# Sample rows packed into one operand, one pass over the attention maps, and values' two parts side by side

## The chip, the cores and the metric

The kernel runs on one core of a Trainium2 chip. The time is that of one execution on the device, in microseconds. TensorE (PE) multiplies matrices out of SBUF into PSUM, VectorE (DVE) and ScalarE (ACT) work element by element, GpSimd (POOL) issues the gathers and scatters of the experts, and SyncE (SP) issues the other DMAs. Each engine runs its own list of instructions in order, and they wait for each other by semaphores.

## What is computed

One layer of a streaming encoder for 512 new prompt tokens (x_prompt) and 32 sample tokens (x_sample) that also see 128 cached keys and values. All is float32. D_MODEL is 1024, with 8 heads of two 64-wide query and key maps and 128-wide values. The part that the change touches:

```python
def diff_attend(q, k, v, mask, lam):
    s = jnp.einsum('bqhmd,bkhmd->bhmqk', q, k).astype(jnp.float32) * ATTN_SCALE
    s = jnp.where(mask, s, -jnp.inf)
    p = jax.nn.softmax(s, axis=-1)
    a = p[:, :, 0] - lam * p[:, :, 1]
    return jnp.einsum('bhqk,bkhv->bqhv', a.astype(v.dtype), v)
...
    h = rms_norm(x, norm_mix_g)
    z = h @ w_in
    u_pool, q, k, v, gate_logits = jnp.split(z, IN_SPLITS, axis=-1)
    q = rope_partial(q.reshape(B, T, N_HEADS, 2, HEAD_DIM), pos)
    k = rope_partial(k.reshape(B, T, N_HEADS, 2, HEAD_DIM), pos)
...
    attn = (rms_norm(attn, subln_g) * (1.0 - lam_init)).reshape(B, T, V_WIDTH)
```

Beside it stand a pooling branch, sigmoid gates for both branches, an output projection, a choice of 2 of 16 experts for each token, and a last norm.

## The kernel before

Every float32 product is made of three matmuls: both operands are split into a high part that TensorE takes exactly (F32R) and the low rest, and `three` adds high x high, high x low and low x high in PSUM. ScalarE copies the high part, VectorE subtracts it from the original to get the low part. Both do this for each chunk of weights that SyncE loads (wh, wl out of rawA), through four slots.

The 544 tokens stand in five tiles of 128. Tiles 0 to 3 are the prompt. Tile 4 holds the last 96 prompt tokens once more and then the 32 sample tokens; only the latter are used of it.

The stages are the norm and its transposes, the pooling branch and its gates, the eight heads, the second gates (gate blocks 0 to 7), the two branches' projections, the output projection, the choice of experts and the experts.

In the stage of the heads, TensorE projects head h (`project(h, j)`, j over 8 rows of weights, in each all five tiles x three matmuls of 384 columns: q, k and v) while the attention of head h-1 runs in between. `turn` transposes q and k of head h-1. `scores(g, t)` makes both maps of query tile t, `turn_probs(g, t)` transposes the combined map, and `values(g, t)` multiplies it with the values, block by block of 128 keys: 1, 2, 3, 4 and 2 blocks for the five tiles, 12 per head. The last two tiles of a head are finished inside the next head's `project(h, 0)` and `project(h, 1)`, ahead of that head's `turn`.

VectorE's `step(g, s)` first combines the maps of tile s-1: reciprocal of both sums, times lambda (L1071), one pass over the first map (L1073), and one that adds the second (L1074). Then it finds the maximum of tile s (nb). Then it makes the low part of the transposed map (atl). Then it clamps the finished tile s-2 and sums its squares (L1090, L1091). ScalarE's `step` squares the finished tile once more at a small scale (bsq), copies it to att, copies the transposed map (ath), and takes the exponentials of tile s with their sums (E, esum). Two sums of squares are kept, for values of ordinary and of huge size.

Around it, for each head: ScalarE copies the five projected tiles to qkv (L737), VectorE applies rotary (L1104 to L1109), ScalarE and VectorE make the high and low parts of v, q and k, and each head's four weight chunks are split at four places (`nxt(3)` to `nxt(6)`). The last head's attention has the gate blocks of TensorE around it in place of a projection. The order is written out by hand; heads 2 to 6 are one loop.

## Time and profile before

| | us |
|---|---|
| median of three runs (943.45 to 947.93) | 946.29 |
| the profiled execution | 945.17 |
| its span | 943.2 |
| TensorE busy | 851.2 |
| VectorE busy | 603.1 |
| ScalarE busy | 505.3 |

The span is the profiled execution from its first to its last instruction; about 2 us of the time lie around it. The granted clock of TensorE is 0.96 of full speed over the whole, and 1.00 in the stage of the heads (132 to 480 us). PE is the list of matmuls, PEld that of their weight loads. A matmul's recorded duration overlaps with its neighbours' because they are pipelined, so the distances between starts tell what one costs. In the timeline a bracket gives the idle time in front of an instruction and who ended it.

### The profile page before, as it was taken

The numbers are of one execution on the slowest core, as the hardware profiler recorded it, in microseconds if no ns is written. First come the engines' busy times: TensorE is split into PE (matmuls) and PEld (weight loads), VectorE is DVE, ScalarE is ACT, GpSimd is POOL, SyncE is SP. The second block draws the span as 40 slices with busy tenths as digits, with TensorE's granted clock in tenths as the row PEclk, the third lists the DMA queues.
The fourth block names the chain that finished last, engine by engine and source line by source line (L and its number), as shares of the span: only waits on it lengthen the run. The fifth ranks groups of instructions, "written<-read, shape, count | busy, mean of one in ns | idle before, by whom it ended". The sixth has DMA issues, their size and how long they took to land.

```text
span 943.2 us, 15744 instructions
## 1 busy us (share of the span) xinstructions
PE 851.2 (90%) x5052; PEld 750.7 (80%) x5052; DVE 603.1 (64%) x1047; ACT 505.3 (54%) x907; POOL 107.6 (11%) x115
## 2 busy tenths in 40 slices
PE   4998999999999999899899998189999999999980
PEld 4998999888888889889898787167777778777760
DVE  6264224676676676566555311658989998998892
ACT  6235213554544544354623212158878887887883
POOL 0000000000000000000000001202432342233221
PEclk8999999999999999999999998579999999999995
DMA  8622133033033023041322914779999999999975
GB/s 247 153 90 65 51 90 84 14 97 96 0 96 96 24 78 97 9 153 43 112 77 82 353 47 158 234 229 315 330 318 333 343 333 346 345 329 327 342 258 202
DMA packets 156131, 164.99 MB, mean 175 GB/s; under 512 B 20877, under 2 KB 140301, under 8 KB 156090
## 3 DMA queue, kind: packets, MB, share of 16 engines
q1 hardware_dynamic: 149706, 152.69, 49.9%
q0 software_dynamic: 6096, 11.17, 4.4%
q10 hardware_dynamic: 288, 0.59, 0.2%
q8 instruction: 25, 0.41, 0.2%
q14 instruction: 16, 0.13, 0.0%
HBM read 153.71 MB, written 19.60 MB: 184 GB/s over the span
## 4 chain that ended last, share of the span: by engine, by line
PE 74%; DVE 8%; DMA 6%; ACT 5%; issue 4%; SPq 2%; ACTq 0%; POOL 0%; DVEq 0%; POOLq 0%
PE ps L1355 23%; PE ps L1357 21%; PE ps L1356 21%; DMA rawM<-in_w_expert_up 2%; PE ps L1494 2%; ACT E L760 2%; SPq L470 2%; PE ps L1663 1%; PE ps L1503 1%; DMA xg<-h_rows,idn 1%; PE ps L1616 1%; DVE wl L951 1%; PE ps L1475 1%; ACT wh L724 1%; DMA gb<-in_norm_mix_g 1%
## 5 line engine op out<-in xcount | busy, mean ns | idle before, releaser
L1298 DVE TENSOR_TENSOR wl<-rawM,wh 128x1024 fp32r<-128x1024 f32 x192 | 227.3, 1221 | 24.2 <-ACT wh L873 23.8
L873 ACT ACTIVATE wh<-rawM 128x1024 fp32r<-128x1024 f32 x195 | 199.2, 1055 | 12.0 <-PE ps L1357 7.9
L1355 PE MATMUL ps<-hTh,wh 128*128 128x272 f32 x448 | 132.6, 296 | 8.1 <-ACT plh L712 3.0
L1357 PE MATMUL ps<-hTh,wl 128*128 128x272 f32 x448 | 131.2, 293 | 0.0
L1356 PE MATMUL ps<-hTl,wh 128*128 128x272 f32 x448 | 130.4, 291 | 0.0
L1355 PE MATMUL ps<-wh,hTh 128*128 128x384 f32 x320 | 116.4, 364 | 8.4 <-ACT qkv L737 6.8
L1355 PE MATMUL ps<-wh,xh 128*128 128x512 f32 x256 | 105.0, 410 | 4.5 <-DVE xl L1321 3.6
L1357 PE MATMUL ps<-wh,hTl 128*128 128x384 f32 x320 | 108.1, 338 | 0.0
L1356 PE MATMUL ps<-wl,hTh 128*128 128x384 f32 x320 | 107.8, 337 | 0.0
L1357 PE MATMUL ps<-wh,xl 128*128 128x512 f32 x256 | 101.9, 398 | 0.0
L1356 PE MATMUL ps<-wl,xh 128*128 128x512 f32 x256 | 101.8, 398 | 0.0
L1355 PEld LDWEIGHTS ps<-hTh,wh 128*128 128x128 f32 x448 | 86.0, 192 | 9.9 <-ACT plh L712 3.2
L951 DVE TENSOR_TENSOR wl<-rawA,wh 128x1024 fp32r<-128x1024 f32 (+2 forms) x41 | 47.2, 1161 | 67.7 <-ACT wh L629 67.7
L1356 PEld LDWEIGHTS ps<-hTl,wh 128*128 128x128 f32 x448 | 86.0, 192 | 0.0
L1357 PEld LDWEIGHTS ps<-hTh,wl 128*128 128x128 f32 x448 | 85.9, 192 | 0.0
L1355 PEld LDWEIGHTS ps<-wh,hTh 128*128 128x128 f32 x320 | 60.1, 188 | 17.4 <-issue 7.5
L629 ACT ACTIVATE wh<-rawA 128x1024 fp32r<-128x1024 f32 (+2 forms) x41 | 40.9, 1014 | 61.3 <-PE ps L1357 59.8
L580 POOL DMA_DIRECT2D h_rows<-hb x4 | 2.4, 590 | 567.1 <-DVE hb L1215 567.1
L1355 PEld LDWEIGHTS ps<-wh,xh 128*128 128x128 f32 x256 | 48.6, 190 | 22.1 <-issue 11.3
L1356 PEld LDWEIGHTS ps<-wl,hTh 128*128 128x128 f32 x320 | 60.4, 189 | 0.0
L1357 PEld LDWEIGHTS ps<-wh,hTl 128*128 128x128 f32 x320 | 60.1, 188 | 0.0
L1357 PEld LDWEIGHTS ps<-wh,xl 128*128 128x128 f32 x256 | 48.5, 189 | 11.8
(255 smaller groups left out, 1679.7 us busy)
## 6 DMA issues: line engine op xcount, KB each, us to landing
rawM<-in_w_expert_gate SPq DMA_DIRECT2D x131, 256.0 KB, 5.9
rawM<-in_w_expert_up SPq DMA_DIRECT2D x131, 256.0 KB, 8.3
rawM<-in_w_expert_down SPq DMA_DIRECT2D x64, 512.0 KB, 9.1
rawA<-in_w_in SPq DMA_DIRECT2D x64, 192.0 KB, 3.0
rawA<-in_w_in SPq DMA_DIRECT2D x20, 512.0 KB, 5.1
rawA<-in_w_attn_branch SPq DMA_DIRECT2D x8, 512.0 KB, 4.5
rawA<-in_w_out SPq DMA_DIRECT2D x8, 512.0 KB, 4.2
x<-in_x_prompt SPq DMA_DIRECT2D x4, 512.0 KB, 6.8
```

The source lines that it names most:

```text
L470: sp.dma_start(d[:, :, m, :], src.rearrange("(k p) n -> p k n", p=P)).then_inc(m_raw[slot], 16)
L629: nc.scalar.activation(split_slot(n)[0][:, 0:w], rawA[:, n % RA, 0:w], ACT.Copy).then_inc(hi_done, 1)
L724: nc.scalar.activation(wh[:, sl, 0:w], rawA[:, sl, 0:w], ACT.Copy).then_inc(hi_done, 1)
L760: ins = nc.scalar.activation(E[s % 2][:, m, 0:n], ps[:, 5 + m, 0:n], ACT.Exp, bias=nb[:, s % 2, m:m + 1], scale=SCALE, accum_out=esum[:, s ...
L873: nc.scalar.activation(wh[:, c % S, :], rawM[:, slot, :], ACT.Copy).then_inc(m_hi, 1)
L951: V.tensor_tensor(l[:, 0:w], rawA[:, n % RA, 0:w], h[:, 0:w].bitcast(F32), ALU.subtract).then_inc(lo_done, 1)
L1298: V.tensor_tensor(wl[:, c % S, :], rawM[:, slot, :], wh[:, c % S, :].bitcast(F32), ALU.subtract).then_inc(m_lo, 1)
L1355: T.matmul(out, sh, mh_, start=start, stop=False, **kw)
L1356: T.matmul(out, sh, ml_, start=False, stop=False, **kw)
L1357: return T.matmul(out, sl, mh_, start=False, stop=stop, **kw)
L1475: ins = T.transpose(ps[:, 5 + m, P * t:P * t + P], qkv[:, t, P * m:P * m + P], id_m)
L1494: ins = T.matmul(ps[:, 5 + m, 0:n], (ql if low_q else qh)[r, col(t)], keys, start=not (low_q or low_k), stop=low_k)
```

## The change

- **Sample rows.** In the head projections tile 4 takes one stationary operand, `dec`. For each row of weights it has 32 columns of the samples' low part and 32 of their high part, and the 128 columns read also take in those of the row before, whose results are not used. Two matmuls (weights' high and low part) replace three; the results of the low part come out in rows 64 to 95 and those of the high part in rows 96 to 127. VectorE adds the two (`join_sample`) before rotary, and ScalarE's copy of v and TensorE's next projection of tile 4 wait for it (`dec_done`). Two copies at the start fill `dec`.
- **Maps.** The first map is no longer divided by its sum. VectorE works out a ratio of both sums and adds the second map in one pass; ScalarE divides when it copies the finished tile out of PSUM.
- **Values.** The high and low parts of v stand side by side (`vv`). The high part of the map goes against both in one matmul of 256 columns, its low part against the high part of v in one of 128. ScalarE copies both halves out (att and clamped). Once a head, in two parts of 3 and 2 tiles, VectorE adds the halves and clamps (`clamp`); ScalarE squares the clamped tiles during the next head (`square`). One sum of squares is left, and the final arithmetic on it is shorter.

```diff
-CLAMP, BIG_SCALE, BIG_SUM = 1.5e18, 2.0 ** -70, 2.0 ** 116
+CLAMP, SQ_SCALE, MAP_SCALE = 2.0 ** 100, 2.0 ** -40, 2.0 ** -9
...
-        vh = hr("vh", [P, NT + 1, P], F32R)
-        vl = hr("vl", [P, NT + 1, P], F32R)
+        vv = hr("vv", [P, NT + 1, 2, P], F32R)
+        vh, vl = vv[:, :, 0, :], vv[:, :, 1, :]
...
+        dec = at("dec", 94 * K, [P, 2 * DEC * (KD + 1)], F32R)
+        dec_lo = dec[:, 2 * DEC:].rearrange("p (k n) -> p k n", k=KD)[:, :, 0:DEC]
+        dec_hi = dec[:, 2 * DEC:].rearrange("p (k n) -> p k n", k=KD)[:, :, DEC:2 * DEC]
...
+                if t == 4:
+                    nc.scalar.activation(dec_hi.rearrange("p (b k) n -> p b k n", b=2), v, ACT.Copy)
...
+            def square(g, t):
+
+                act.wait_ge(cl_done, 2 * g + (1 if t < 3 else 2))
+                nc.scalar.activation(clamped[:, t, :], clamped[:, t, :], ACT.Square, scale=SQ_SCALE,
+                                     accum_out=ssb[:, t, bass.ds(g, 1)]).then_inc(sq_done, 1)
+
             def step(g, s):
 
+                if s < NT and not (isinstance(g, int) and g == 0):
+                    square(g - 1, s)
                 if s >= 2:
                     act.wait_ge(av_mm, NT * g + s - 1)
-                    nc.scalar.activation(bsq[:], ps[:, 7, 0:P], ACT.Square, scale=BIG_SCALE,
-                                         accum_out=ssb[:, s - 2, bass.ds(g, 1)])
-                    nc.scalar.activation(att[:, s - 2, g, :], ps[:, 7, 0:P], ACT.Copy).then_inc(av_ev, 1)
+                    act.wait_ge(sq_done, NT * g + s - 1)
+                    nc.scalar.activation(att[:, s - 2, g, :], ps[:, 7, 0:P], ACT.Copy, scale=rinv[:, s % 2, 0:1])
+                    nc.scalar.activation(clamped[:, s - 2, :], ps[:, 7, P:2 * P], ACT.Copy,
+                                         scale=rinv[:, s % 2, 0:1]).then_inc(av_ev, 1)
...
+            for t in range(3):
+                square(HEADS - 1, t)
             step(HEADS - 1, NT + 1)
             gate_block(5)
+            for t in range(3, NT):
+                square(HEADS - 1, t)
...
+            per_head = 3 + 4 * NT
+            per_tail = 4
+
+            def clamp(g, part, lk):
+
+                tiles = slice(0, 3) if part == 0 else slice(3, NT)
+                dve.wait_ge(av_ev, NT * g + (3 if part == 0 else NT))
+                dve.wait_ge(sq_done, NT * (g + 1))
+                lk(V.tensor_tensor(att[:, tiles, g, :], att[:, tiles, g, :], clamped[:, tiles, :], ALU.add))
+                V.tensor_scalar(clamped[:, tiles, :], att[:, tiles, g, :], CLAMP, -CLAMP, ALU.min,
+                                ALU.max).then_inc(cl_done, 1)
+
+            def step(g, s, lk, join=None):
 
                 if 1 <= s <= NT:
                     t = s - 1
                     n = P * (t + 1) if t < 4 else 2 * P
                     dve.wait_ge(exp_done, NT * g + s)
                     lk(V.reciprocal(rinv[:, t % 2, :], esum[:, t % 2, :]))
-                    V.tensor_tensor(rinv[:, t % 2, 1:2], rinv[:, t % 2, 1:2], nlam[:], ALU.mult)
                     a0, a1 = E[t % 2][:, 0, 0:n], E[t % 2][:, 1, 0:n]
-                    lk(V.tensor_scalar(a0, a0, rinv[:, t % 2, 0:1], None, ALU.mult))
-                    V.scalar_tensor_tensor(out=a0, in0=a1, scalar=rinv[:, t % 2, 1:2], in1=a0,
+                    lk(V.scalar_tensor_tensor(out=ratio[:, t % 2:t % 2 + 1], in0=esum[:, t % 2, 0:1],
+                                              scalar=rinv[:, t % 2, 1:2], in1=nlam[:], op0=ALU.mult, op1=ALU.mult))
+                    V.scalar_tensor_tensor(out=a0, in0=a1, scalar=ratio[:, t % 2:t % 2 + 1], in1=a0,
                                            op0=ALU.mult, op1=ALU.add).then_inc(am_done, 1)
+                if join is not None:
+                    join_sample(join)
                 if s < NT:
                     n = P * (s + 1) if s < 4 else 2 * P
                     dve.wait_ge(sc_mm, NT * g + s + 1)
                     unseen = ps[0:HD, 5:7, n - CHUNK:n] if s < 4 else ps[:, 5:7, 0:LAST]
                     lk(V.memset(unseen, NEG))
                     lk(V.tensor_reduce(mx[:, s % 2, :], ps[:, 5:7, 0:n], AX.X, ALU.max))
-                    V.tensor_scalar(nb[:, s % 2, :], mx[:, s % 2, :], -SCALE, None, ALU.mult).then_inc(nb_done, 1)
+                    V.scalar_tensor_tensor(out=nb[:, s % 2, :], in0=mx[:, s % 2, :], scalar=-SCALE, in1=shift[:],
+                                           op0=ALU.mult, op1=ALU.add).then_inc(nb_done, 1)
                 if 1 <= s <= NT:
                     kb = s if s < NT else 2
                     dve.wait_ge(ath_done, NT * g + s)
                     V.tensor_tensor(atl[:, 0:kb, :], ps[:, 7, 0:kb * P].rearrange("p (k n) -> p k n", k=kb),
                                     ath[:, 0:kb, :].bitcast(F32), ALU.subtract).then_inc(atl_done, 1)
-                if s >= 2:
-                    dve.wait_ge(av_ev, NT * g + s - 1)
-                    lk(V.tensor_scalar(asq[:], att[:, s - 2, g, :], CLAMP, -CLAMP, ALU.min, ALU.max))
-                    ins = V.scalar_tensor_tensor(out=asq[:], in0=asq[:], scalar=1.0,
-                                                 in1=asq[:], op0=ALU.mult, op1=ALU.mult,
-                                                 accum_out=ssa[:, s - 2, bass.ds(g, 1)])
-                    lk(ins)
+                if s == NT:
+                    clamp(g, 0, lk)
+
+            def join_sample(g):
+
+                dve.wait_ge(acc_ev, NT * (g + 1))
+                V.tensor_tensor(qkv[LAST:P, 4, :], ps[2 * DEC:LAST, 4, 0:384], qkv[LAST:P, 4, :],
+                                ALU.add).then_inc(dec_done, 1)
...
                 nxt(3)
+                if not (isinstance(g, int) and g == 0):
+                    clamp(g - 1, 1, lk)
                 nxt(4)
...
-                if not first:
-                    step(h - 2, NT, lk)
+                if first:
+                    join_sample(h - 1)
+                else:
+                    step(h - 2, NT, lk, h - 1)
                 rope(h - 1, lk)
-                if not first:
-                    step(h - 2, NT + 1, lk)
                 attend(h - 1, lambda k: lo_head(k % 4, n + k, WH if k == 3 else w_next), lk)
                 assert links[0] == (d1 if first else per_head)
...
-            big, one = BIG_SUM / (BIG_SCALE ** -2), 2.0 ** 128 * BIG_SCALE ** 2
-            link(V.tensor_scalar(fin[:], ssb[:], big, None, ALU.is_ge))
-            link(V.tensor_scalar(isb[:], ssb[:], one, 2.0 ** -40 * BIG_SCALE ** -2 / P, ALU.min, ALU.mult))
-            link(V.tensor_tensor(isb[:], isb[:], fin[:], ALU.mult))
-            link(V.tensor_scalar(rsa[:], ssa[:], 2.0 ** -40 / P, 2.0 ** -40 * EPS, ALU.mult, ALU.add))
-            link(V.tensor_scalar(fin[:], fin[:], -1.0, 1.0, ALU.mult, ALU.add))
-            link(V.tensor_tensor(rsa[:], rsa[:], fin[:], ALU.mult))
-            link(V.tensor_tensor(rsa[:], rsa[:], isb[:], ALU.add))
-            V.tensor_scalar(fin[:], ssb[:], one, 2.0 ** -20, ALU.is_lt, ALU.mult).then_inc(ms_done, 1)
+            clamp(HEADS - 1, 1, link)
+            full = 2.0 ** 128 * SQ_SCALE ** 2
+            dve.wait_ge(sq_done, NT * (HEADS + 1))
+            link(V.tensor_scalar(rsa[:], ssb[:], full, 1.0 / SQ_SCALE, ALU.min, ALU.mult))
+            V.tensor_scalar(fin[:], ssb[:], full, 2.0 ** -20, ALU.is_lt, ALU.mult)
+            V.tensor_scalar(rsa[:], rsa[:], P * EPS * SQ_SCALE, None, ALU.add).then_inc(ms_done, 1)
...
+                            if t == 4:
+                                pe.wait_ge(dec_done, h)
+                    if t < 4:
+                        ins = three(ps[:, t, 0:384], hTh[:, j, col(t)], hTl[:, j, col(t)], wh[:, sl, wc], wl[:, sl, wc],
+                                    j == 0, j == KD - 1)
+                    else:
+                        both = dec[:, 2 * DEC * j:2 * DEC * j + P]
+                        T.matmul(ps[:, t, 0:384], both, wh[:, sl, wc], start=j == 0, stop=False)
+                        ins = T.matmul(ps[:, t, 0:384], both, wl[:, sl, wc], start=False, stop=j == KD - 1)
...
-                    ins = three(ps[:, 7, 0:P], ath[:, kb, :], atl[:, kb, :], vh[:, v, :], vl[:, v, :],
-                                kb == 0, kb == len(vs) - 1)
+                    T.matmul(ps[:, 7, 0:2 * P], ath[:, kb, :], vv[:, v], start=kb == 0, stop=False)
+                    ins = T.matmul(ps[:, 7, 0:P], atl[:, kb, :], vv[:, v, 0, :], start=False, stop=kb == len(vs) - 1)
```

VectorE, from the loop's end on: the last step of head 5, up to rotary of head 6. Before (E is the pair of maps, rot the rotary's scratch), then now:

```order
L1070 RECIPROCAL rinv<-esum 128x2
L1071 TENSOR_TENSOR rinv<-rinv,nlam 128x1
L1073 TENSOR_SCALAR E_80<-E_80,rinv 128x256
L1074 SCALAR_TENSOR_TENSOR E_80<-E_80,rinv 128x256
L1086 TENSOR_TENSOR atl<-ps,ath 128x256
L1090 TENSOR_SCALAR asq<-att 128x128
L1091 SCALAR_TENSOR_TENSOR asq,ssa<-asq 128x128
L1104 TENSOR_TENSOR rot<-qkv,cst 128x160
```

```order
L1103 RECIPROCAL rinv<-esum 128x2
L1105 SCALAR_TENSOR_TENSOR ratio<-esum,rinv,nlam 128x1
L1107 SCALAR_TENSOR_TENSOR E_81<-E_81,ratio 128x256
L1130 TENSOR_TENSOR qkv<-ps,qkv 32x384
L1122 TENSOR_TENSOR atl<-ps,ath 128x256
L1093 TENSOR_TENSOR att<-att,clamped 128x3x128
L1094 TENSOR_SCALAR clamped<-att 128x384
L1141 TENSOR_TENSOR rot<-qkv,cst 128x160
```

The pass L1073 is gone, the joining of qkv stands ahead of atl, and the addition and clamp of three tiles stand where one tile was clamped and squared.

VectorE, in the same head, between the low parts of k and the first maximum. Before, then now:

```order
L1121 TENSOR_TENSOR ktl<-ps,kth 128x256
L1058 TENSOR_TENSOR wl<-rawA,wh 128x768
L1058 TENSOR_TENSOR wl<-rawA,wh 128x1024
L1080 MEMSET ps 64x2x64
L1081 TENSOR_REDUCE mx<-ps 128x2
L1082 TENSOR_SCALAR nb<-mx 128x2
```

```order
L1158 TENSOR_TENSOR ktl<-ps,kth 128x256
L1082 TENSOR_TENSOR wl<-rawA,wh 128x768
L1093 TENSOR_TENSOR att<-att,clamped 128x2x128
L1094 TENSOR_SCALAR clamped<-att 128x256
L1082 TENSOR_TENSOR wl<-rawA,wh 128x1024
L1115 MEMSET ps 64x2x64
L1116 TENSOR_REDUCE mx<-ps 128x2
L1117 SCALAR_TENSOR_TENSOR nb<-mx,shift 128x2
```

The addition and clamp of the previous head's two last tiles now stand between the two weight splits, ahead of nb.

TensorE, in the loop over the heads, from tile 1 of a head's first projection (wh, wl against hTh, hTl) to the values of tile 3 of the head two before; they have four blocks, of which the first is shown. Before, then now:

```order
L1356 MATMUL ps<-wl,hTh 128x384
L1357 MATMUL ps<-wh,hTl 128x384
L1507 ISA
L1355 MATMUL ps<-vh,ath 128x128
L1356 MATMUL ps<-vl,ath 128x128
L1357 MATMUL ps<-vh,atl 128x128
```

```order
L1390 MATMUL ps<-wl,hTh 128x384
L1391 MATMUL ps<-wh,hTl 128x384
L1548 ISA
L1551 MATMUL ps<-vv,ath 128x256
L1552 MATMUL ps<-vv,atl 128x128
```

A block of keys has two matmuls in place of three, one of them twice as wide.

## Rows read from the trace of the kernel before

**Rows 1.** Page: busy us, share and instructions by engine; then the chain's shares.
```profile
PE 851.2 (90%) x5052; PEld 750.7 (80%) x5052; DVE 603.1 (64%) x1047; ACT 505.3 (54%) x907; POOL 107.6 (11%) x115
...
PE 74%; DVE 8%; DMA 6%; ACT 5%; issue 4%; SPq 2%; ACTq 0%; POOL 0%; DVEq 0%; POOLq 0%
```

**Rows 2.** Timeline of weight loads (start, us, engine, line, operation): 384, 128, 272 columns.
```profile
261.06 0.19 PEld L1355 LDWEIGHTS ps<-wh,hTh 128*128 128x128 f32 x1
...
261.93 0.19 PEld L1357 LDWEIGHTS ps<-wh,hTl 128*128 128x128 f32 x1
...
286.02 0.19 PEld L1357 LDWEIGHTS ps<-vh,atl 128*128 128x128 f32 x1
...
287.03 0.19 PEld L1357 LDWEIGHTS ps<-vh,atl 128*128 128x128 f32 x1
...
396.12 0.19 PEld L1357 LDWEIGHTS ps<-hTh,wl 128*128 128x128 f32 x1
...
399.14 0.19 PEld L1357 LDWEIGHTS ps<-hTh,wl 128*128 128x128 f32 x1
```

**Rows 3.** Timeline of weight loads, one turn; in brackets idle time before, and releaser.
```profile
258.38 0.86 PEld L1475 LDWEIGHTS ps<-cst,qkv 128*128 128x128 f32 x8 [0.28 <-DVE qkv L1109]
...
262.40 0.19 PEld L1494 LDWEIGHTS ps<-kh,qh 64*128 64x128 f32 x2 [0.28 <-DVE ktl L1121]
...
265.82 0.19 PEld L1494 LDWEIGHTS ps<-kh,qh 64*128 64x128 f32 x2 [0.35 <-ACT E L760]
...
269.62 0.19 PEld L1494 LDWEIGHTS ps<-kh,qh 64*128 64x128 f32 x2
...
276.47 0.31 PEld L1503 LDWEIGHTS ps<-cst,E 128*128 128x128 f32 x3 [0.54 <-DVE E L1074]
...
278.57 0.19 PEld L1355 LDWEIGHTS ps<-vh,ath 128*128 128x128 f32 x1 [0.30 <-DVE atl L1086]
...
284.74 0.19 PEld L1355 LDWEIGHTS ps<-wh,hTh 128*128 128x128 f32 x1 [1.44 <-ACT qkv L737]
...
288.66 0.32 PEld L1503 LDWEIGHTS ps<-cst,E 128*128 128x128 f32 x2
...
292.48 0.20 PEld L1475 LDWEIGHTS ps<-cst,qkv 128*128 128x128 f32 x2 [0.28 <-DVE qkv L1109]
```

**Rows 4.** Timeline of VectorE, 255 to 293 us.
```profile
259.43 0.82 DVE L1114 TENSOR_TENSOR vl<-qkv,vh 128x640 fp32r<-128x640 f32 x1
...
262.26 1.82 DVE L1058 TENSOR_TENSOR wl<-rawA,wh 128x768 fp32r<-128x768 f32 x2
...
264.76 0.17 DVE L1082 TENSOR_SCALAR nb<-mx 128x2 f32<-128x2 f32 x1
...
275.08 0.16 DVE L1070 RECIPROCAL rinv<-esum 128x2 f32<-128x2 f32 x1
275.27 0.16 DVE L1071 TENSOR_TENSOR rinv<-rinv,nlam 128x1 f32<-128x1 f32 x1
275.35 0.41 DVE L1073 TENSOR_SCALAR E<-E,rinv 128x384 f32<-128x384 f32 x1
275.80 0.62 DVE L1074 SCALAR_TENSOR_TENSOR E<-E,rinv 128x384 f32<-128x384 f32 x1
...
290.01 0.22 DVE L1090 TENSOR_SCALAR asq<-att 128x128 f32 x1
...
290.80 0.33 DVE L1104 TENSOR_TENSOR rot<-qkv,cst 128x160 f32<-128x160 f32 x1
```

**Rows 5.** Timeline of ScalarE in the same turn.
```profile
269.82 0.28 ACT L743 ACTIVATE bsq<-ps 128x128 f32<-128x128 f32 x1 [0.77 <-PE ps L1357]
...
284.20 2.02 ACT L737 ACTIVATE qkv<-ps 128x384 f32<-128x384 f32 x5
```

**Rows 6.** Timeline of weight loads, last head, beside the gate blocks.
```profile
412.26 0.19 PEld L1494 LDWEIGHTS ps<-kh,qh 64*128 64x128 f32 x2 [0.90 <-ACT E L760]
...
425.39 0.31 PEld L1503 LDWEIGHTS ps<-cst,E 128*128 128x128 f32 x3 [1.76 <-DVE E L1074]
```

More of the change, by code:

```diff
@@ L148, in build @@
         rinv = small("rinv", [P, 2, 2])
-        ssa = small("ssa", [P, NT, HEADS])
         rsa = small("rsa", [P, NT, HEADS])
         ssb = small("ssb", [P, NT, HEADS])
+        shift = small("shift", [P, 2])
+        ratio = small("ratio", [P, 2])
         wgt = small("wgt", [P, NT, 2])
@@ L238, in build @@
         rot = at("rot", 203 * K, [P, 4, 160])
-        isb = at("isb", 203 * K, [P, NT, HEADS])
         fin = at("fin", 203 * K + 160, [P, NT, HEADS])
-        asq = at("asq", 203 * K + 2560, [P, P])
-        bsq = at("bsq", 203 * K + 3072, [P, P])
+        clamped = at("clamped", 96 * K + 256, [P, NT, P])
         ckv = at("ckv", 203 * K + 3584, [P, 2, P])
@@ L278, in build @@
                              "sel_done", "pos_mm", "hot_done", "list_mm", "id_done", "xg_clear"))
[L279 removed]
+        eps_done, warm_chain, dec_done = sem("eps_done"), sem("warm_chain"), sem("dec_done")
         cum_done, gb_mm, gb_ev, gate_done = sem("cum_done"), sem("gate_mm"), sem("gate_ev"), sem("gate_done")
@@ L770, in attend @@
                 act.wait_ge(ckv_in, 32 * (g + 1))
+                act.wait_ge(dec_done, g + 1)
                 nc.scalar.activation(vh[:, 0:NT, :], qkv[:, :, 2 * P:3 * P], ACT.Copy)
@@ L799, in gate_block @@
                                      ps[:, 2 * (b % 2):2 * (b % 2) + 2, 0:HALF], ACT.Copy).then_inc(gb_ev, 1)
+            act.sem_inc(sq_done, NT)
             split_to(H0 + 6)
@@ L962, in _ @@
             V.memset(U[:, :, 0:BUF], 0.0).then_inc(pad_done, 1)
+            V.memset(shift[:, 0:1], math.log(MAP_SCALE))
+            V.memset(shift[:, 1:2], 0.0)
+            V.memset(dec[:, 0:2 * DEC].bitcast(F32), 0.0)
             V.memset(idi[:, ROWS:ROWS + 2], 0)
@@ L987, in _ @@
                 v, oh, ol = rows_lo(t, X_BANKS[t])
+                if t == 4:
+                    V.tensor_tensor(dec_lo.rearrange("p (b k) n -> p b k n", b=2), v, oh, ALU.subtract)
                 V.tensor_tensor(ol, v, oh, ALU.subtract).then_inc(xt_lo, 1)
@@ L1102, in rope @@
                 tmp = [rot[:, r, :].rearrange("p (t g d) -> p t g d", t=NT, g=4) for r in range(4)]
-                dve.wait_ge(acc_ev, NT * (g + 1))
+                dve.wait_ge(dec_done, g + 1)
                 V.tensor_tensor(tmp[0], x1, cos, ALU.mult)
@@ L1458, in project @@
                             pe.wait_ge(acc_ev, NT * (h - 1) + t + 1)
-                    ins = three(ps[:, t, 0:384], hTh[:, j, col(t)], hTl[:, j, col(t)], wh[:, sl, wc], wl[:, sl, wc],
-                                j == 0, j == KD - 1)
+                            if t == 4:
+                                pe.wait_ge(dec_done, h)
[6 more added lines that the diff above has]
+                        ins = T.matmul(ps[:, t, 0:384], both, wl[:, sl, wc], start=False, stop=j == KD - 1)
                     if j == KD - 1 and t < 4:
@@ L1587, in _ @@
                     pe.wait_ge(acc_ev, NT * HEADS)
+                    pe.wait_ge(dec_done, HEADS)
                 if t < 2:
```

12 lines of the change are left out of this document (3 added, 9 removed).

## The prediction

> **What bounds the kernel now.** I read the busy shares and the chain that ended last first [rows 1]: TensorE is busy 90% of the span and carries 74% of the chain, so an instruction taken off it is worth its distance to the next one, unless TensorE stands waiting just behind it. The change touches only the stage of the eight heads and its tail in the gate blocks, from about 129 to 453 us. Everything behind it is gated by that stage's results or by each other, so it should shift as a block.
>
> Next I read the starts of TensorE's weight loads, which give the distance of two matmuls; the listed durations overlap and can't be summed. Five steps of 384-column matmuls take 0.87 us, 0.174 each; nine steps of 128-column ones 1.01 us, 0.112 each; 24 steps of 272-column ones 3.02 us, 0.126 each [rows 2].
>
> Last I read one turn of the head loop, with what TensorE waited for [rows 3]. It takes 34.10 us (258.38 to 292.48) and holds six waits with a releaser, of 0.28 to 1.44 us; the profile marks two short ones more as issue, which stay. They divide it into legs, and the forecast is made leg by leg. A leg that ends in a wait is as long as its chain through VectorE and ScalarE, and matmuls removed inside it only lengthen the wait; in a leg without a wait they count in full.
>
> **What is removed and added, each by itself.**
> - Projection: one 384-column matmul fewer for each of 8 heads x 8 rows of weights, 64 x 0.174 = 11.1 us.
> - Values: a block of keys takes three 128-column matmuls now, 0.336 us. Afterwards it takes one of 256 columns and one of 128. The 256-column one is not in the trace; it lies between 0.112 and 0.126 and is nearest to the 272-column row, so I take 0.12, and a block costs 0.232. A block saves 0.104 (bounds 0.098 and 0.112); 96 blocks make 10.0 us. Together 21.1 us of TensorE work.
> - Maps on VectorE: the full pass TENSOR_SCALAR over the first map goes. In its place the tiny ratio is awaited before the last pass. For 384 keys the distance from L1071 to L1074 is 0.53; a tiny op that is waited for takes 0.19 (L1070 to L1071), so 0.33 is saved [rows 4]. For 512 keys it is a little more.
> - Clamp and square: VectorE's two passes per tile go. In their place come an addition and a clamp over 3 tiles (part 0) and over 2 tiles (part 1). A TENSOR_TENSOR is 0.33 at 160 elements and 0.82 at 640, 1.02 ns an element, so 0.56 at 384 and 0.43 at 256. A TENSOR_SCALAR is 0.22 at 128 and 0.41 at 384, so 0.32 at 256 [rows 4]. Between two such passes lies 0.04 (from L1073's end to L1074); I allow up to 0.15 for the register work that comes with the head's index. So part 0 is about 1.0 and part 1 about 0.8 us.
> - ScalarE: a square, reading back its sum, and a copy stand between L743 at 269.82 and the end of the tile, two operations of 0.28 or so. Now there are two copies, and the square is done a head later in ScalarE's idle time, such as the 0.77 us in front of L743 [rows 5]. It costs nothing there. If ScalarE had no such gap, it would be 40 x 0.28 = 11 us.
> - The joining of the sample's two parts (32 x 384 out of PSUM, about 0.55 us by the same TENSOR_TENSOR line) starts when the five copies of qkv end, 284.20 + 2.02 = 286.2. Its first reader on TensorE is tile 4 of the next projection, three matmuls ahead of L1503 at 288.66, thus 288.1. The 1.3 us between them cover it, even less 0.4 for the shorter values ahead. Rotary waits behind it but starts only at 290.80. Cost 0.
> - The two extra copies of the normalised sample rows at the start, and the memsets: two small operations beside other tiles' matmuls, 0.
>
> **The legs of one head**, by [rows 3] and [rows 4]:
> - Turn to first scores, 4.02 us: ends in a wait for VectorE (ktl). The chain is transposes, ScalarE's copies, VectorE's low parts, and none of it changes. The removed matmul lengthens the wait. 0.
> - First to second scores, 3.42 us: ends in a wait for ScalarE's E, and this is VectorE's chain: two weight splits (1.82 us from 262.26), then the maximum, nb at 264.76, then exp. Part 1 of the clamp is put between the two splits, as VectorE's order shows. +0.80 (bounds 0.6 and 1.1). This applies to the 7 heads that have a predecessor.
> - Second to third scores, 3.80 us: no wait. One matmul and one block: -0.28.
> - Third scores to the next head, 15.12 us. There is a wait of 0.54 for E of the third map, so its chain sets the pace, and it loses 0.33. Then the values wait 0.30 for atl, which follows the same VectorE chain: again 0.33 earlier in all. From there three blocks save 0.31, and the rest (scores, transposes, ath, exp, weight split, qkv copy, ending in the 1.44 wait) hangs on them at fixed distances. -0.64. The removed matmuls of three projections are lost.
> - Next head to the last map's transposes, 3.92 us: one matmul and four blocks, no wait within but that at its start. -0.59.
> - From there to the next turn, 3.82 us: ends in a wait of 0.28 for rotary. The chain is ath, atl, clamp passes, rotary. The old clamp and square take 290.01 to 290.80, 0.79; part 0 takes 1.0 [rows 4]. +0.20, and the matmul and two blocks are lost to the wait.
>
> A turn of the loop thus saves 0.28 + 0.64 + 0.59 - 0.80 - 0.20 = 0.51 us, where its TensorE work shrinks by 8 x 0.174 + 12 x 0.104 = 2.64.
>
> **The sum.** Clamp part 1: +0.80 x 7 = +5.6. Part 0 ahead of rotary: +0.20 x 6 = +1.2. Second to third scores: 7 x 0.28 = 1.96 off. Third scores to next head: 7 x 0.64 = 4.48 off. Next head to last transposes: 6 x 0.59 = 3.54 off. Head 0 and the first two projections of head 1 have no such wait: 10 x 0.174 = 1.74 off. In the gate blocks TensorE has the long matmul runs between, so what is left of head 6 (six blocks) gives 0.62 off. Head 7 gives one block, then 0.33 at its wait for E, which is 1.76 us there [rows 6], then nine blocks: 0.10 + 0.33 + 0.94 = 1.37 off. Its share of part 1 is already counted, in front of L1494 at 412.26 [rows 6]. The tail (clamp, squares, root, scaling of att) has the two last gate blocks over it, 96 x 0.126 = 12 us, and it grows by about a microsecond: 0. In all 6.8 - 13.7 = -6.9 us.
>
> The profiled execution took 945.17 us, so 938.3. The three runs have the median 946.29, 1.1 above it; forecast against them **939.4 us**. With part 1 at 0.6 or 1.1 and part 0 at +0.1 or +0.4 the sum is -8.9 or -3.6.
>
> The Trainium skill, "VectorE: DVE Perf Modes" (section on the TRN2 errata), prices a matmul at max(60, 6 + columns) cycles, which is 56 ns for 128 columns and 109 for 256. By it three small ones would equal one wide and one small, and the values would give nothing. The row of 0.112 us per 128-column matmul speaks against it; "TensorE: Matmul & The Clock Gate" (section LDWEIGHTS) gives a load as columns / 1.2 ns, 107 ns, which fits the row.
>
> **The rivals.**
> - *The whole of the TensorE work arrives*: -21.1 us, 925. It needs the chains to have slack that the six waits deny, or part 1 to fall into idle time of VectorE. For it: VectorE is busy only 64% of the span [rows 1]. Against it: it goes from the two splits to nb without a pause [rows 4]. Half of it (a part 1 that VectorE can start early) would be -9.5 to -14. 0.13 for more than -9.5.
> - *The wide matmul saves nothing*: if 256 columns cost two steps of 0.112, each block saves 0. The blocks that count are 7 + 21 + 24 + 6 + 10 = 68, 7.1 us, and the sum is +0.2, 946.5. The 272-column row contradicts it. 0.05.
> - *The additions are dearer*, by 0.2 to 0.5 us a place (register work in the loop, strided reads): over 13 places -4.3 to -0.3; 942 to 946. 0.20, and with the one above 0.25.
> - *Slower*: VectorE's inserted clamp passes become the loop's new bound. 6.9 us over 13 places is 0.53 us each; from there on the change loses. At twice their price (1.6 and 2.0) they add 11.2 + 7.2 = 18.4 against 13.7, +4.7, 951. For it: they stand in the two legs that already end in a wait. Against: the rows of the same kinds of pass scatter by a few hundredths. 0.06.
>
> **How the numbers follow.** The forecast, with its own range -9.5 to -3.6, has 0.56; what is faster 0.13, dearer or without gain 0.25, slower 0.06. Half a per cent is 4.7 us, about what a measurement here can tell from no change. Of the forecast 0.50 lies beyond it, and so does the first rival: faster 0.63. Same 0.31, slower 0.06. The range leaves out about a tenth on each side: 932 to 945.5.
>
> **What the profile afterwards would show.** A turn of the loop of 33.6 us. First to second scores 4.2 us, with the wait for E at 1.3 instead of 0.35, and the clamp of part 1 between two wl rows. A turn-to-scores leg still at 4.0 with a wait of 0.45. Steps of 0.12 in the values. The wait for rotary at 0.9. If the waits stay at their old size and the turn takes 31.5, the first rival holds; if the loop takes over 34.1, the last. The forecast is wrong if the clamp passes don't delay nb, or if the wait in front of the next head grows by more than the 0.17 of the one matmul ahead of it.

## The result, and the profile after

| | before | after |
|---|---|---|
| median, us (14 runs each) | 945.58 (943.45 to 947.93) | 941.37 (935.90 to 942.78) |
| ratio after to before | | 0.9945, 95% interval 0.9932 to 0.9958 |
| profiled execution, us (its span) | 945.17 (943.2) | 941.4 (939.5) |

The kernel is 0.55% faster, 4.2 us by the medians. The forecast of 939.4 is 2.0 us below the measured median, which lies inside the range of 932 to 945.5, and "faster" was right. The route there was right only in part: three terms were missed, and one of the two largest (1.5 us each) is not in the sum at all.

TensorE's work shrank as computed. The page of after, busy time and share by engine, answers to the first line of [rows 1]:

```profile
PE 833.0 (89%) x4892; PEld 731.0 (78%) x4892; DVE 592.1 (63%) x926; ACT 518.9 (55%) x948; POOL 107.8 (11%) x115
```

There are 160 matmuls fewer: 64 of the projection and 96 of the values. ScalarE gained 13.6 us of work and VectorE lost 11.0. By the distances of [rows 2] the 160 are worth 21.1 us; the kernel became 4.2 us faster. Where the rest went shows in the sums of TensorE's waits inside the stage. First before, then after (what the weight loads waited for: us in total, number of waits, longest), from 150 to 480 us; the groups that hardly differ between the two are left out:

```profile
PEld ps L1355 <- ACT qkv L737: 9.3, 6, 2.1
...
PEld ps L1503 <- DVE E L1074: 6.2, 8, 1.8
PEld ps L1494 <- ACT E L760: 3.6, 8, 0.9
...
PEld ps L1355 <- DVE atl L1086: 2.3, 8, 0.3
PEld ps L1494 <- DVE ktl L1121: 2.3, 8, 0.3
PEld ps L1475 <- DVE qkv L1109: 1.4, 5, 0.3
```

```profile
PEld ps L1535 <- ACT E L773: 11.4, 16, 1.5
PEld ps L1389 <- ACT qkv L741: 10.3, 6, 2.2
...
PEld ps L1544 <- DVE E L1107: 6.6, 8, 1.6
PEld ps L1516 <- DVE qkv L1146: 5.5, 6, 0.9
PEld ps L1535 <- DVE ktl L1158: 3.5, 8, 0.5
PEld ps L1551 <- DVE atl L1122: 3.5, 8, 0.5
```

The six sources add up to 25.1 us before and 40.8 after, so TensorE waits 15.7 us more. Two things are in this sum: removed matmuls that stood ahead of a wait, and the clamp passes, which make two chains of VectorE longer. The experiments part them below. The biggest rise, 3.6 to 11.4, is at the scores (L1494, now L1535). Most of it is the wait in front of the second scores, which grew from 0.35 to 1.18 in the turn shown; the count has also doubled, and the eight new waits are of about 0.26.

One turn of the head loop in after, weight loads with the idle time before them, answers to [rows 3] row by row. It has one wait more, in the seventh row:

```profile
254.83 0.86 PEld L1516 LDWEIGHTS ps<-cst,qkv 128*128 128x128 f32 x8 [0.92 <-DVE qkv L1146]
...
258.85 0.19 PEld L1535 LDWEIGHTS ps<-kh,qh 64*128 64x128 f32 x2 [0.46 <-DVE ktl L1158]
...
262.92 0.19 PEld L1535 LDWEIGHTS ps<-kh,qh 64*128 64x128 f32 x2 [1.18 <-ACT E L773]
...
266.40 0.19 PEld L1535 LDWEIGHTS ps<-kh,qh 64*128 64x128 f32 x2
...
272.96 0.31 PEld L1544 LDWEIGHTS ps<-cst,E 128*128 128x128 f32 x3 [0.65 <-DVE E L1107]
...
275.06 0.19 PEld L1551 LDWEIGHTS ps<-vv,ath 128*128 128x128 f32 x1 [0.47 <-DVE atl L1122]
...
276.08 0.19 PEld L1535 LDWEIGHTS ps<-kth,qh 64*128 64x128 f32 x2 [0.26 <-ACT E L773]
...
281.09 0.19 PEld L1389 LDWEIGHTS ps<-wh,hTh 128*128 128x128 f32 x1 [1.63 <-ACT qkv L741]
...
284.39 0.31 PEld L1544 LDWEIGHTS ps<-cst,E 128*128 128x128 f32 x2
...
288.46 0.86 PEld L1516 LDWEIGHTS ps<-cst,qkv 128*128 128x128 f32 x8 [0.92 <-DVE qkv L1146]
```

| leg of the turn, us | before | after | difference | forecast |
|---|---|---|---|---|
| turn to first scores | 4.02 | 4.02 | 0 | 0 |
| first to second scores | 3.42 | 4.07 | +0.65 | +0.80 |
| second to third scores | 3.80 | 3.48 | -0.32 | -0.28 |
| third scores to next head | 15.12 | 14.69 | -0.43 | -0.64 |
| next head to last map's transposes | 3.92 | 3.30 | -0.62 | -0.59 |
| from there to the turn | 3.82 | 4.07 | +0.25 | +0.20 |
| the turn | 34.10 | 33.63 | -0.47 | -0.51 |

The leg that missed most ends in the wait for qkv, 1.44 before and 1.63 after; the new wait of 0.26 stands in its middle, in front of the scores of kth.

The two edits on VectorE read like this in after (start, duration; the rows answer to [rows 4]). Part 0 of the clamp, over three tiles, stands ahead of rotary; part 1, over two, between the two weight splits:

```profile
252.11 0.55 DVE L1093 TENSOR_TENSOR att<-att,clamped 128x384 f32 x1
252.69 0.55 DVE L1094 TENSOR_SCALAR clamped<-att 128x384 f32 x1
253.16 0.32 DVE L1141 TENSOR_TENSOR rot<-qkv,cst 128x160 f32<-128x160 f32 x1
...
258.72 0.95 DVE L1082 TENSOR_TENSOR wl<-rawA,wh 128x768 fp32r<-128x768 f32 x1
259.58 0.42 DVE L1093 TENSOR_TENSOR att<-att,clamped 128x256 f32 x1
260.03 0.29 DVE L1094 TENSOR_SCALAR clamped<-att 128x256 f32 x1
260.24 0.95 DVE L1082 TENSOR_TENSOR wl<-rawA,wh 128x768 fp32r<-128x768 f32 x1
...
261.87 0.16 DVE L1117 SCALAR_TENSOR_TENSOR nb<-mx,shift 128x2 f32<-128x2 f32 x1
```

From the first addition to rotary 1.05 us pass, against 0.79 for the old clamp and square. Part 1 pushes the second split from 259.58 to 260.24, 0.66 us, and nb with it.

One thing in after is in no leg of this turn: a stretch of half clock. Windows of 5 us (busy us and count by engine, then TensorE's granted clock), first of after, then of before:

```profile
380.00:385.00 5.00, 3.12 (x20) 2.79 (x19) 3.08 (x8) 4.35 (x11) 0.00 (x0) 0.95 0.00 0
385.00:390.00 5.00, 5.00 (x32) 5.00 (x31) 0.34 (x1) 0.62 (x2) 0.00 (x0) 0.71 0.00 0
```

```profile
385.00:390.00 5.00, 3.26 (x22) 2.94 (x22) 3.62 (x11) 4.36 (x11) 0.00 (x0) 1.00 0.01 2
```

and the weight loads of after in it, at the start of the gate blocks, behind the wait for the last head's qkv:

```profile
383.45 0.19 PEld L1389 LDWEIGHTS ps<-hTh,wh 128*128 128x128 f32 x1 [2.21 <-ACT qkv L741]
...
385.09 0.33 PEld L1391 LDWEIGHTS ps<-hTh,wl 128*128 128x128 f32 x1
385.32 0.33 PEld L1389 LDWEIGHTS ps<-hTh,wh 128*128 128x128 f32 x1
...
398.65 0.91 PEld L1516 LDWEIGHTS ps<-cst,qkv 128*128 128x128 f32 x8
```

A step of 272 columns takes 0.23 us here and 0.126 elsewhere: the lower of the two levels, 1.2 against 2.4 GHz, for some 3.4 us. From 383.45 to the last head's turn it is 15.20 us, where 13.68 was to be expected from the runs below. This costs 1.52 us.

Over the whole stage, from its first matmul to the transposes of att, it is 323.37 us before and 318.67 after, -4.70, or about -6.2 without the half clock, where the sum said -6.9. What lies behind the stage took 490.0 us before and 490.9 after. After has two such stretches there (granted clock 0.66 in the window from 455 us and 0.74 in that from 515), before has one (0.73 in the window from 460).

### The profile page after: what moved, and what is told of

It reads as the page before. It is cut to its first block, busy times and chain, and to the rows that moved or that the text cites. A ratio compares the mean times of both kernels' runs of the same rounds, so it can differ in the third digit from the quotient of the medians.

```text
span 939.5 us, 15321 instructions
## 1 busy us (share of the span) xinstructions
PE 833.0 (89%) x4892; PEld 731.0 (78%) x4892; DVE 592.1 (63%) x926; ACT 518.9 (55%) x948; POOL 107.8 (11%) x115
## 4 chain that ended last, share of the span: by engine, by line
PE 43%; DVE 5%; DMA 5%; SPq 2%; ACT 2%; issue 2%; ACTq 0%; POOL 0%; POOLq 0%; DVEq 0%
PE ps L1389 13%; PE ps L1391 13%; PE ps L1390 13%; DMA rawM<-in_w_expert_up 2%; SPq L472 2%; PE ps L1705 1%; DMA xg<-h_rows,idn 1%; PE ps L1658 1%; DVE wl L970 1%; DVE ob L1379 1%; DMA sum_rows<-yb,ydn 1%; PE ps L1725 1%; PE ps L1652 1%; DVE hTl L1222 1%; DVE wl L1332 1%
## 5 line engine op out<-in xcount | busy, mean ns | idle before, releaser
L1389 PE MATMUL ps<-wh,hTh 128*128 128x384 f32 x256 | 94.3, 369 | 9.4 <-ACT qkv L741 7.9
L1389 PEld LDWEIGHTS ps<-hTh,wh 128*128 128x128 f32 x448 | 86.8, 194 | 10.1 <-ACT plh L716 3.2
L1391 PE MATMUL ps<-wh,hTl 128*128 128x384 f32 x256 | 86.4, 337 | 0.0
L1390 PE MATMUL ps<-wl,hTh 128*128 128x384 f32 x256 | 86.2, 337 | 0.0
L1389 PEld LDWEIGHTS ps<-wh,hTh 128*128 128x128 f32 x256 | 48.1, 188 | 18.6 <-ACT qkv L741 8.1
L1390 PEld LDWEIGHTS ps<-wl,xh 128*128 128x128 f32 x256 | 48.7, 190 | 10.3
L773 ACT ACTIVATE E<-ps,nb 128x256 f32<-128x256 f32 (+3 forms) x80 | 40.4, 513 | 26.1 <-DVE nb L1117 26.1
```

The source lines that it names most:

```text
L773: ins = nc.scalar.activation(E[s % 2][:, m, 0:n], ps[:, 5 + m, 0:n], ACT.Exp, bias=nb[:, s % 2, m:m + 1], scale=SCALE, accum_out=esum[:, s ...
L1389: T.matmul(out, sh, mh_, start=start, stop=False, **kw)
L1390: T.matmul(out, sh, ml_, start=False, stop=False, **kw)
L1391: return T.matmul(out, sl, mh_, start=False, stop=stop, **kw)
```

## The experiments

**The theory**: the two parts of the clamp cost what the legs show, because each stands in a chain of VectorE that TensorE waits for; and the removed matmuls count only in legs that end in no wait. **The rivals**: the legs were stretched by something else (register work of the loop, ScalarE's added copies), so that moving the clamp gives nothing; or the wait would be taken over at once by the next chain.

**Part 1 moved.** The clamp of the last two tiles goes behind the first maximum and its nb, so that exp no longer waits for it.

```
                 nxt(3)
-                if not (isinstance(g, int) and g == 0):
-                    clamp(g - 1, 1, lk)
                 nxt(4)
...
                     step(g, s, lk)
+                    if s == 0 and not (isinstance(g, int) and g == 0):
+                        clamp(g - 1, 1, lk)
```

> The changed kernel with one edit: part 1 of the clamp (two tiles) stands after the first maximum of the head in place of between the two weight splits. Theory (chains): in the changed kernel the leg from the first to the second scores takes 4.07 us, with a wait for E of 1.18, because 0.66 us of clamp passes lie ahead of nb. Moved into VectorE's idle 0.87 us behind nb they should delay nothing: the leg falls to 3.42, seven times, the loop's turn from 33.67 to about 33.0, the whole by 4.5 us, to 937. Rival (TensorE's own work sets the leg, or the time goes elsewhere, to the clock): the leg stays near 4.0 and the time at 941.

Measured: 936.69 us (936.41 to 937.00), ratio to before 0.9895, interval 0.9866 to 0.9924. The weight loads of this kernel at the first two scores:

```profile
258.51 0.19 PEld L1535 LDWEIGHTS ps<-kh,qh 64*128 64x128 f32 x2 [0.47 <-DVE ktl L1158]
...
261.92 0.19 PEld L1535 LDWEIGHTS ps<-kh,qh 64*128 64x128 f32 x2 [0.53 <-ACT E L773]
```

The leg from first to second scores is 3.41 again, as before the change (3.42), and the wait in front of it is 0.53, down from 1.18. The turn is 33.04. The theory holds for this leg to 0.01 us.

**Part 0 moved** behind rotary, in all heads.

```
-                if s == NT:
-                    clamp(g, 0, lk)
...
                 rope(h - 1, lk)
+                if not first:
+                    clamp(h - 2, 0, lk)
                 attend(h - 1, ...)
```

> The changed kernel with one edit: part 0 of the clamp (three tiles, 1.05 us) stands behind rotary in place of ahead of it. Theory (chains): TensorE waits 0.92 us for rotary ahead of its transposes; the wait vanishes and six heads save 0.9 each, while the passes fall into VectorE's idle 0.66 and 0.62 us behind rotary. The turn falls to about 32.8, the whole by 5.4, to 936. Rival: the passes now delay the low part of v and with it ktl, so that the wait ahead of the first scores grows from 0.46 by as much as the other shrinks, and nothing is gained.

Measured: 936.83 us, ratio 0.9898 (0.9869 to 0.9927), turn 33.06.

```profile
252.76 0.97 PEld L1518 LDWEIGHTS ps<-cst,qkv 128*128 128x128 f32 x8
...
257.05 0.19 PEld L1537 LDWEIGHTS ps<-kh,qh 64*128 64x128 f32 x2 [0.63 <-DVE ktl L1156]
...
261.12 0.19 PEld L1537 LDWEIGHTS ps<-kh,qh 64*128 64x128 f32 x2 [1.20 <-ACT E L773]
```

The wait of 0.92 at the turn is gone. But the next leg grew from 4.02 to 4.29, ending in 0.63 for ktl: about a third of the gain is handed on to the next chain, in which the clamp now stands. The step gives 0.6 us a turn, not 0.9. Here theory and second rival are both right in part.

**Both moved** together.

> Both moves together. Theory (chains): the two legs are separate, so the gains add: 4.5 + 5.4 = 9.9 us off the changed kernel, 931.5, ratio to the kernel before 0.985. Rival (another engine takes over when both waits are gone): clearly less than the sum, about 5 us.

Measured: 932.07 us (931.76 to 933.05), ratio 0.9845 (0.9816 to 0.9874), turn 32.39. The gains add: 33.63 less 0.59 and 0.57 is 32.47. The moved parts have no new wait of their own.

The sums of TensorE's waits, over the same window as above, part what the 15.7 us are. The two that changed most:

```profile
PEld ps L1537 <- ACT E L773: 6.9, 16, 0.9
...
PEld ps L1537 <- DVE ktl L1156: 4.3, 8, 0.6
```

The wait for rotary (5.5 in after) is gone. The six sources add up to 31.8 us here, against 40.8 in after: 9.0 of the 15.7 us came from where the clamp stood, and 6.7 are left with the same matmuls.

**The projection alone undone.** Tile 4 has three matmuls again; the joining stays as an instruction of the same size (a maximum of two equal operands).

```
-                    if t < 4:
+                    if t < 5:
                         ins = three(ps[:, t, 0:384], ...
...
-                V.tensor_tensor(qkv[LAST:P, 4, :], ps[2 * DEC:LAST, 4, 0:384], qkv[LAST:P, 4, :],
-                                ALU.add).then_inc(dec_done, 1)
+                V.tensor_tensor(qkv[LAST:P, 4, :], ps[LAST:P, 4, 0:384], qkv[LAST:P, 4, :],
+                                ALU.max).then_inc(dec_done, 1)
```

> The changed kernel with the packing of the sample rows undone: tile 4 of each head projection is again three matmuls out of the two parts of the normalised rows; the joining instruction stays, at the same size, as a maximum of two equal operands. Theory (legs): only those of the 64 matmuls come back that stand in legs without a wait: 10 at the start, 7 in the leg of the second scores, 6 in that of the last map, 23 x 0.174 = 4.0 us, to 945.4; the waits in front of the turn, the first scores, the second scores and the next head shrink by 0.17 each. Rival (all TensorE work counts): 64 x 0.174 = 11.1 us slower, 952.

Measured: 943.06 us (10 runs), ratio 0.9973 (0.9958 to 0.9988), turn 34.01.

```profile
223.60 0.86 PEld L1516 LDWEIGHTS ps<-cst,qkv 128*128 128x128 f32 x8 [0.75 <-DVE qkv L1146]
...
227.62 0.19 PEld L1535 LDWEIGHTS ps<-kh,qh 64*128 64x128 f32 x2 [0.29 <-DVE ktl L1158]
...
231.69 0.19 PEld L1535 LDWEIGHTS ps<-kh,qh 64*128 64x128 f32 x2 [1.00 <-ACT E L773]
```

Each of the three waits is 0.17 to 0.18 shorter than in after (0.92, 0.46, 1.18) and its leg is unchanged: 4.02, 4.07. That is one 384-column matmul going into a wait, seen directly. The stage is 4.13 us longer than that of after without its half clock, where 4.0 was expected, of the 11.1 us that the 64 matmuls are worth. The medians differ by only 1.7. That fits this kernel's trace, which has no half clock at the gate blocks.

**The wide matmul alone undone.** The halves of the values' operand get a 128-column matmul each, into the same places.

```
-                    T.matmul(ps[:, 7, 0:2 * P], ath[:, kb, :], vv[:, v], start=kb == 0, stop=False)
+                    T.matmul(ps[:, 7, 0:P], ath[:, kb, :], vv[:, v, 0, :], start=kb == 0, stop=False)
+                    T.matmul(ps[:, 7, P:2 * P], ath[:, kb, :], vv[:, v, 1, :], start=False, ...)
```

> The changed kernel with only the wide matmul undone: the high part of the map goes against v's high and low parts in two matmuls of 128 columns, into the same places; everything else stays. Theory: a block costs 0.336 us again in place of 0.232. That counts in full where no wait follows: one block in the leg of the second scores (7 heads), four in that of the last map (7 heads), and what the last head has; in the leg up to the next head the three blocks are mostly swallowed by the 0.26 us wait for E ahead of the last scores, which appeared with the change: of 0.31 only 0.05 comes back. Sum 7 x 0.10 + 7 x 0.42 + 7 x 0.05 + 0.2 + 1.0 = 5.2 us slower than the changed kernel, about 945, and the 0.26 us wait is gone. Rival (the wide matmul gains nothing, 256 columns take two steps): same time as the changed kernel, and steps of 0.22 in it.

Measured: 944.56 us (10 runs), ratio 0.9985 (0.9972 to 0.9997), turn 34.34; the stage is 6.0 us longer than after's without the half clock, where 5.2 was expected. So the rival, no gain, is refuted. The place of the missed term, weight loads of this kernel:

```profile
242.76 0.19 PEld L1551 LDWEIGHTS ps<-vv,ath 128*128 128x128 f32 x1 [0.47 <-DVE atl L1122]
...
243.91 0.18 PEld L1535 LDWEIGHTS ps<-kth,qh 64*128 64x128 f32 x2
```

With narrow blocks the 0.26 in front of the kth scores is gone and the way from values to scores takes 1.15 us, exactly as before the change (278.57 to 279.72); in after it is 1.02. Three blocks give 0.13 there, not 0.31. So the wide matmul itself gives its full 0.104 a block, and the wait for E takes 0.18 of 0.31.

The third part of the change, the pass over the first map that VectorE no longer makes, was not undone by itself; its worth is only read from the legs.

**A split moved on both engines.** If the loop is bound by the chains, then shortening the one with the longest wait (qkv, 1.62) should give more than any matmul. On top of both moves, the fourth weight split goes behind the five copies of qkv on ScalarE, and behind the joining on VectorE.

```
-                attend(h - 1, lambda k: hi_head(...))
+                attend(h - 1, lambda k: None if k == 6 else hi_head(...))
                 evacuate(h)
+                hi_head(2, n + 6, h + 1, w_next)
...
                     join_sample(join)
+                    lo_head(2, H0 + 4 * join + 6, ...)
```

> Both clamp moves, and the fourth weight split of each head (0.74 us of ScalarE) stands behind the five copies of qkv in place of ahead of them, VectorE's half of it behind the joining. Theory (chains): TensorE's wait of 1.62 us ahead of the next head is ScalarE's chain of exponentials, split and first copy; it shrinks by 0.74, seven times, 5.2 us off the kernel with both moves (932.1), 927; the turn falls from 32.39 to about 31.7. Rival: the split then delays the map's transposed copy or the rotary chain, and the wait moves there.

Measured: 925.59 us (924.04 to 925.79), ratio 0.9777 (0.9762 to 0.9792), turn 31.63. This is the fastest kernel of the case, ahead of before and after.

```profile
242.88 0.19 PEld L1393 LDWEIGHTS ps<-wh,hTh 128*128 128x128 f32 x1 [0.90 <-ACT qkv L741]
```

The wait fell from 1.62 to 0.90 us. With the same 4892 matmuls as after it takes 15.8 us less by the medians (941.37 to 925.59); the stage is 13.8 us shorter than after's without the half clock. Against both moves alone it is 6.5 us; 7 turns of 0.76 make 5.3 of them, and the trace of both moves had a stretch of half clock at 375 us that this one lacks.

**One split more.** Another weight split goes behind the first maximum, part 1 of the clamp one step later.

> As the kernel before it in this list, and in the first seven heads the second weight split stands behind the first maximum on VectorE and behind the first exponentials on ScalarE, with part 1 of the clamp one step later still. Theory (chains): nb comes 0.9 us earlier, the wait of 0.52 ahead of the second scores vanishes, seven times, 3.6 us more off, about 923.5. Rival: the split and the combining of the first map now fill VectorE between nb and the map's transposes, which wait instead; no gain.

Measured: 928.88 us (925.65 to 929.38), ratio 0.9815 (0.9802 to 0.9829), turn 31.83, slower by 3.3 than without by the medians. In the traces the stage is 1.7 us longer, 7 turns of 0.20 among them; what the rest is was not shown.

```profile
227.46 0.14 PEld L1555 LDWEIGHTS ps<-cst,E 128*128 128x128 f32 x1 [0.29 <-DVE E L1111]
...
229.61 0.19 PEld L1546 LDWEIGHTS ps<-kh,qh 64*128 64x128 f32 x2 [0.38 <-ACT E L773]
```

The wait for E in front of the second scores (0.51) is gone, and two new ones of 0.29 and 0.38 stand behind it. Here the rival holds: the moved work only changes which tile waits for it.

**The half clock.** After, unchanged, once more:

> The changed kernel unchanged, profiled once more. In its first profile the granted clock stood at half for 3.4 us from 384.4 on, right behind a wait of 2.2 us, and once more at 515 us, and the matmuls there had distances of 0.227 in place of 0.126. Theory (these dips come after waits but not each time): the same waits, the same distances elsewhere, and the dips in other places, so that the stage of the heads ends up to 1.5 us earlier or later. Rival (the kernel's order causes it): the same dips at 384 and 515.

Measured: 942.61 us. The wait is 2.21 again, and the way to the turn is 15.20 again, from 383.16 to 398.36. The second stretch is not there: the wait in front of it is 2.57 in both traces (at 512.64 and 513.72), and the granted clock behind it is 0.74 in the first and 1.00 in the second. So each side is right for one of the two places.

Part 1 moved has the same wait (2.22) at the gate blocks but 13.68 behind it; both moves has 2.23 and 15.23. Is it the length of the wait, or when it falls? Two kernels shift everything by a little: 8 and 20 additional matmuls of 384 columns ahead of head 0, whose results are overwritten.

```
+                    if j == 0 and t == 0 and isinstance(h, int) and h == 0:
+                        for _ in range(8):
+                            T.matmul(ps[:, t, 0:384], hTh[:, j, col(t)], wh[:, sl, wc], start=True, stop=True)
```

> The changed kernel with 8 additional matmuls of 384 columns ahead of the first head projection, whose results are overwritten: the stage of the heads comes 8 x 0.174 = 1.4 us later, with the same waits. Both profiles of the changed kernel have the granted clock at half for some 3 us right behind the wait of 2.2 us for the first gate block. Theory (the dip depends on when the wait falls, not on its length alone): with the shift the dip is gone or lies elsewhere, and from that wait to the last head's turn it takes 13.7 us in place of 15.2. Rival (the wait's length decides): 15.2 again. Each kernel with one move of a clamp kept the wait at 2.2 and had no dip, which speaks for the theory.

> The same with 20 additional matmuls, 3.5 us later. Theory: as above, dip or no dip by where the wait falls, 13.7 or 15.2 us, independent of the run before it. Rival: 15.2 in both.

Measured: 942.13 and 942.63 us. With 8 additional matmuls:

```profile
384.45 0.19 PEld L1389 LDWEIGHTS ps<-hTh,wh 128*128 128x128 f32 x1 [2.21 <-ACT qkv L741]
...
398.14 0.91 PEld L1519 LDWEIGHTS ps<-cst,qkv 128*128 128x128 f32 x8
```

With 20 the wait is 2.21 as well, at 387.43, and the turn comes at 401.11. So the same wait has 13.69 and 13.68 us behind it, and no half clock there. The length of the wait alone doesn't decide it. Whether the shift removed it is not shown: each shifted kernel ran once, and one and the same program differs from execution to execution, as the second stretch above does. So do the 14 runs of after: in six of them the mean granted clock was 0.961 to 0.964 and they took 935.90 to 939.57 us, in the other eight it was 0.956 to 0.959 and they took 941.33 to 942.78.

The totals of the two didn't fall. With 8 additional matmuls the part behind the stage takes 492.2 us, with a longer stretch of half clock from 455 us on (granted clock 0.50 in the window from 455, 0.82 in the next). With 20 it takes 489.7, without one, but the stage has 3.5 us of additional matmuls. What sets the moment stays open.

## Why the prediction was right, and where it was not

*TensorE's removed work, 21.1 us.* Right in size. The wide matmul and its neighbour take 0.23 a block (two blocks in 0.45 in the last head, where 0.464 was forecast), and each 384-column one 0.17 to 0.18.

*What of it arrives.* The rule of the legs held: in five of six legs the differences are within 0.15 of the forecast, and the projection alone undone shows the matmul vanishing into three waits one after another. Undone one at a time, the two parts bring back 4.1 and 6.0 us of the stage, 10.1 of the 21.1. So the first rival, that all 21.1 us arrive, is refuted.

*Part 1 of the clamp.* The sum had +0.80 for each of 7 heads; it was 0.66 in VectorE's order and +0.65 in the leg. The term of 5.6 us was 4.6, on the low side of its bounds. The 0.15 allowed for register work between the passes wasn't there: the second starts 0.45 after the first, which lasts 0.42.

*Part 0 ahead of rotary.* +0.25 against +0.20, 1.5 us for 6 turns in place of 1.2. The clamp over three tiles took 0.55 and not the 0.41 of the 384-element TENSOR_SCALAR of [rows 4], while that over two took 0.29, about 0.32 as expected. Rotary still started 0.47 after it, so the dearer pass hardly shows. The Trainium skill, "VectorE: DVE Perf Modes" (section What auto-detection actually checks), says that an operation with one source in SBUF takes its mode with two results a cycle if the outermost dimensions of source and destination are both even, or equal. The three-tile source is 3 x 128 and its destination 384 in a row, the two-tile one 2 x 128: the rows agree with the rule, 1.43 ns an element against 1.13. No run changed the shape by itself.

*Third scores to the next head.* The forecast had -0.64 and it was -0.43, over 7 heads 1.5 us. The step that failed is the sentence that the rest "hangs on them at fixed distances". Of its pieces, up to the maps' transposes it was -0.29 (0.33 forecast: from the ratio to the pass it takes 0.25, where 0.19 was reckoned), to the values 0, from the values to the kth scores -0.13 (0.31 forecast), and from there to the next head -0.01. The kth scores overwrite what exp of the fourth tile reads. In the timeline of ScalarE of after, the second half of this exp and the reading of its sum:

```profile
275.26 0.68 ACT L773 ACTIVATE E<-ps,nb 128x512 f32<-128x512 f32 x1
275.83 0.20 ACT L773 ACTIVATION_READ_ACCUMULATOR E<-ps,nb 128x1 f32 x1
```

It ends at 276.03, and the scores start at 276.08. Exp of this tile starts at 274.58, released by nb (before: 278.09), and the values, released by atl, 0.48 us later in both kernels: the two chains of VectorE move together. Before, the scores came at 279.72, 0.18 after its end at 279.54, so the slack of the chain was 0.18 less what a hand-over takes, and a saving of 0.31 couldn't fit into it. The number was in the trace and was not looked at, since no wait stood there. The sign named for being wrong, a wait in front of the next head that grows by more than 0.17, came in by 0.02 (1.44 to 1.63); the way from the kth scores to the next head is the same to 0.01, so this growth is the one matmul, and the sign would not have found the failed step.

*The head without a predecessor.* Right: 26.16 us before, 24.40 after, -1.76 against -1.74.

*Joining, ScalarE, memsets.* Put at nothing, and nothing in the traces speaks against it. The joining took 0.56 and started at 282.59, and no TensorE wait names it; no run moved ScalarE's square or left it out.

*The half clock at the gate blocks.* Not in the sum, and no rival spoke of it. It costs 1.5 us in the stage, and after has one more than before in the part behind the stage, which is 0.8 us longer; that it is the cause there was not shown. The trace of before has such a stretch too (granted clock 0.73 in the window from 460 us), so a term "these move" with a size of 1.5 us either way could have been given from it.

In sum the stage's forecast of -6.9 stands against -6.2 without the half clock: part 1 cost 1.0 less than expected, the leg to the next head gave 1.5 less, the rest is tenths. That the two nearly cancel is luck. With the half clock it is -4.7, and with the parts ahead of and behind the stage -3.8 in the profiled execution. The prediction's own arithmetic has two slips, neither of which changes it: its bounds sum to -8.9, and the text below them uses -9.5; and the dearer additions end at -0.4, not at -0.3.

## What to carry to other kernels

Divide a loop into legs at TensorE's waits before pricing removed matmuls: one that stands ahead of a wait only lengthens the wait, and a leg without a wait still has a slack to be read, from the end of what it depends on to its start. Here about half of 21 us of removed TensorE work reached the time, and passes added in front of two waits took much of that back, so that 4.2 us were left. Moving three pieces of VectorE and ScalarE work behind the operation that TensorE waits for gave 15.8 more with not one matmul fewer. Moved work pays as long as no other tile waits for it; here the next piece moved gave two new waits and lost 3.3 by the medians.

## What the runs showed of the hardware

Short stretches with TensorE's granted clock at half come behind waits of 2 to 3 us, but not behind each. Behind the wait of 2.2 us at the first gate block there is one in three traces (after twice, both moves) and none in five (each move alone, the wide matmul undone, the two shifts). Behind the wait of 2.57 us near 513 us one trace of after has one and the other has none. One of some 3.4 us costs about 1.5 us where TensorE has no slack.

The Trainium skill, "TensorE: Matmul & The Clock Gate" (section What's actually happening), says that the gate's beat isn't set by the kernel's start, so that the moment of a change varies. The second stretch of after, there once and not there once, fits that, and so does the wide range of after's runs (935.90 to 942.78, where part 1 moved has 936.41 to 937.00). That both traces of after have the stretch at the gate blocks speaks rather for a fixed one. No run here decides. Kernels that differ by 1 or 2 us are therefore better compared by their legs than by their medians.

The 256-column matmul with a 128-column one takes 0.23 us at full clock, where two 128-column ones take 0.224: in this stream, with a weight load for each matmul, 256 columns cost about the same step as 128.
